# Block 2's output product by token block, with residual, norm and transposes beside it, and the first MLP product begun with the first token half

## What is computed

```
    h = rms_norm(x, norm_mix[l])
    x = x + hybrid_mixer(h, ...)          # ends with: return y @ w_out
    h = rms_norm(x, norm_mlp[l])
    x = x + jnp.square(jax.nn.relu(h @ w_up[l])) @ w_down[l]
    return rms_norm(x, norm_final)
```

## Time and profile before

| | us |
|---|---|
| median of 3 runs | 3333.64 (3332.24 to 3339.71) |
| the profiled execution | 3333.65 |
| its span in the trace | 3331.8 |
| PE busy | 3049.6 (92%) |
| DVE busy | 1804.0 (54%) |
| ACT busy | 1091.8 (33%) |
| POOL busy | 956.8 (29%) |

### The profile page before, as it was taken

How to read it: one execution, slowest core, us unless ns; L and a number is a source line. 1 busy time by engine, 2 the same in 40 slices (tenths; PEclk the granted TensorE clock), 3 DMA queues, 4 the chain that set the end, 5 groups by cost and what they waited for, 6 DMA issues and landing times.

```text
span 3331.8 us, 49239 instructions
## 1 busy us (share of the span) xinstructions
PE 3049.6 (92%) x20177; PEld 1927.5 (58%) x20394; DVE 1804.0 (54%) x2991; ACT 1091.8 (33%) x1912; POOL 956.8 (29%) x958
## 2 busy tenths in 40 slices
PE   7989988998779969997999999999998899999997
PEld 7449773885439646873555655654656644444443
DVE  2584892666489973767365265365353333333334
ACT  2352651664356634654122122222221310000001
POOL 2301383002203571012423322323222233333330
PEclk9997999999899989998999999999898899999998
DMA  7313231002102321003101111111102111111101
GB/s 241 126 57 118 77 137 54 30 11 102 67 13 77 115 89 49 14 28 128 51 26 38 51 38 39 38 39 51 39 13 102 39 51 51 51 51 51 51 26 57
DMA packets 49168, 207.19 MB, mean 62 GB/s; under 512 B 4488, under 2 KB 9776, under 8 KB 32304
## 3 DMA queue, kind: packets, MB, share of 16 engines
q1 hardware_dynamic: 42288, 195.63, 16.5%
q10 hardware_dynamic: 6656, 8.39, 0.8%
HBM read 187.22 MB, written 16.79 MB: 61 GB/s over the span
## 4 chain that ended last, share of the span: by engine, by line
PE 75%; DVE 15%; issue 4%; ACT 3%; DMA 1%; POOL 1%; DVEq 0%; SPq 0%; ACTq 0%; POOLq 0%
PE big L270 17%; PE big L271 17%; PE big L269 17%; PE banks L269 4%; PE banks L270 4%; PE banks L271 4%; PE banks L994 3%; DVE arena L1614 2%; PE banks L861 1%; DVE arena L1835 1%; PE big L548 1%; PE banks L548 1%; DVE arena L2004 1%; DVE arena L1817 1%; DVE arena L1949 1%
## 5 line engine op out<-in xcount | busy, mean ns | idle before, releaser
L511 POOL CAST w_hi<-stage 128x512 bf16<-128x512 f32 x432 | 284.7, 702 | 1880.5 <-PE big L271 1142.6
L518 POOL TENSOR_TENSOR w_lo<-stage,w_hi 128x512 bf16<-128x512 f32 x520 | 676.4, 1333 | 396.9 <-ACT w_hi L1129 396.2
L270 PE MATMUL big<-ht_lo,w_hi 128*128 128x512 bf16 x1381 | 526.6, 381 | 21.1 <-DVE ht_lo L1515 18.7
L271 PE MATMUL big<-ht_hi,w_lo 128*128 128x512 bf16 x1380 | 525.8, 381 | 1.4
L269 PE MATMUL big<-ht_hi,w_hi 128*128 128x512 bf16 x1359 | 517.7, 381 | 1.5
L269 PE MATMUL big<-w_hi,ht_hi 128*128 128x256 bf16 (+1 forms) x1274 | 383.8, 301 | 22.5 <-POOL w_lo L518 9.6
L271 PE MATMUL big<-w_hi,ht_lo 128*128 128x256 bf16 (+1 forms) x1276 | 384.2, 301 | 0.5 <-issue 0.2
L270 PE MATMUL big<-w_lo,ht_hi 128*128 128x256 bf16 (+1 forms) x1274 | 383.7, 301 | 0.6 <-issue 0.4
L269 PEld LDWEIGHTS big<-ht_hi,w_hi 128*128 128x128 bf16 x1408 | 140.1, 100 | 180.3 <-DVE ht_lo L1515 19.1
L271 PEld LDWEIGHTS big<-ht_hi,w_lo 128*128 128x128 bf16 x1408 | 138.4, 98 | 168.3 <-issue 3.8
L270 PEld LDWEIGHTS big<-ht_lo,w_hi 128*128 128x128 bf16 x1408 | 138.4, 98 | 162.1 <-issue 6.0
(11 more groups left out here) (319 smaller groups left out, 6095.8 us busy)
## 6 DMA issues: line engine op xcount, KB each, us to landing
stage<-in_w SPq DMA_DIRECT2D x130, 1024.0 KB, 4.8
arena<-in_w_ada SPq DMA_DIRECT2D x48, 512.0 KB, 4.2
arena<-in_x SPq DMA_DIRECT2D x16, 512.0 KB, 7.0
xs<-arena SPq DMA_DIRECT2D x16, 512.0 KB, 2.6
arena<-xs SPq DMA_DIRECT2D x16, 512.0 KB, 7.9
gt<-arena ACTq DMA_DIRECT2D x16, 256.0 KB, 2.5
arena<-gt ACTq DMA_DIRECT2D x16, 256.0 KB, 2.6
out_x<-arena SPq DMA_DIRECT2D x8, 512.0 KB, 2.6
```

What stands on the lines that cost most here:

```text
L270: pe.matmul(out, ah, bl, start=False, stop=False)
L271: return pe.matmul(out, al, bh, start=False, stop=stop)
L511: pool.tensor_copy(w_hi[:, n % RING, c0:c1], stage[:, n % RAW_RING, c0:c1]).then_inc(s_w_hi_split, mark(s_w_hi_split, n, q))
L518: ins = pool.tensor_tensor(w_lo[:, n % RING, c0:c1], stage[:, n % RAW_RING, c0:c1], w_hi[:, n % RING, c0:c1], ALU.subtract)
```

## The change

The output product goes by token block. Chunks o0 to o3 now hold a quarter of `w_out` each as 512 rows x 512 columns (in place of 1024 x 256), so that a token block's PSUM tile holds its whole row of 1024 outputs and takes 48 matmuls of 512 columns. Token blocks 0 and 1 are done first together: for both, the six k that belong to b = 0 to 2 come before the wait for the last tile of `Y2`, the two k of b = 3 behind it. Blocks 2 to 7 follow one by one. DVE adds a block's row, then normalises the block before it, into a new place (`X_TOK3`, since `Y2` is still read).

The first token half is turned in the middle of block 6, the second in the middle of up0, which is done in four parts (column tile 0 and 1 of the first token half, then of the second). The transposes go to the `c2` banks. The passes behind them are new and fewer: ACT scales from PSUM straight to `ht_hi`, DVE makes `ht_lo` from PSUM, gain and `ht_hi` in one instruction. On both engines the first half's passes stand ahead of block 5's step. SP's reload of x moves from behind o2's load to behind up1's. up0's tiles are in pool `big`; up1 starts pool `mlp` at its first tile.

```
-                if n == CHUNK_AT[(2, "o2")]:
+                if n == CHUNK_AT[(2, "up1")]:
 
                     sp.wait_ge(s_hgrn_dve, when(s_hgrn_dve, "y2_f", 3, 1))
...
@@
+            def turn_x(l, half, kps):
+
+                if kps[0] == 0:
+                    for j in range(4):
+                        pe.wait_ge(s_xn, when(s_xn, l, half * 4 + j))
+                for kp in kps:
+                    g = take(pe, "c2", "hx", l, half, kp)
+                    for kk in range(2):
+                        for j in range(4):
+                            k = 2 * kp + kk
+                            ins = pe.transpose(g[:, kk * 512 + j * P:kk * 512 + (j + 1) * P],
+                                               x_tok(l)[:, half * 4 + j, k * P:(k + 1) * P], ident)
+                    ins.then_inc(s_gemm, mark(s_gemm, "hx", l, half, kp))
+
+            def first_gemm(l, name, keys):
...
+                part(0, 0)
+                turn_x(l, 1, (0, 1))
+                part(1, 0)
+                turn_x(l, 1, (2, 3))
+                part(0, 1)
+                part(1, 1)
+                chunk_used(l if l < LAYERS else 2, name, s_gemm)
+
+            def out_tokens(l, names, yT, first_two, ready):
...
+                def part(t, g, p, c, ks=range(4)):
+                    w = chunk(l, names[p][c], 4)
+                    for k in ks:
+                        ins = mm3(pe, g[:, c * 512:(c + 1) * 512], [x[:, 4 * p + k, t * P:(t + 1) * P] for x in yT],
+                                  [x[:, k, :] for x in w], p == 0 and k == 0, p == 1 and k == 3)
+                    return ins
+
+                first = [take(pe, "big", "y", l, t) for t in range(2)]
+                first_two(part, first)
+                for t in range(2, NT):
+                    ready(t)
+                    g = take(pe, "big", "y", l, t)
+                    for q, (p, c) in enumerate(((0, 0), (0, 1), (1, 0), (1, 1))):
+                        if t == 6 and q < 3:
+                            turn_x(nl, 0, ((0, 1), (2,), (3,))[q])
+                        ins = part(t, g, p, c)
+                        if t == NT - 1 and q < 3:
+                            ins.then_inc(s_gemm, mark(s_gemm, "y_part", l, p, c))
+                            chunk_used(l, names[p][c], s_gemm)
+                    ins.then_inc(s_gemm, mark(s_gemm, "y", l, t))
+                chunk_used(l, names[1][1], s_gemm)
@@
-            pe.wait_ge(s_hgrn_dve, when(s_hgrn_dve, "y2_lo", 3, 1))
-            out_proj(2, Y2)
-            transpose_x(3)
-            pe.wait_ge(s_ht_lo, when(s_ht_lo, "all", 3))
-            for c, j in MLP:
+
+            def first_two(part, g):
+                pe.wait_ge(s_hgrn_dve, when(s_hgrn_dve, "y2_lo", 2, 1))
+                for p, ks in ((0, range(4)), (1, range(2))):
+                    for c in range(2):
+                        pe.wait_ge(s_w_split, when(s_w_split, CHUNK_AT[(2, f"o{2 * p + c}")]))
+                        for t in range(2):
+                            part(t, g[t], p, c, ks)
+                pe.wait_ge(s_hgrn_dve, when(s_hgrn_dve, "y2_lo", 3, 1))
+                for t in range(2):
+                    for c in range(2):
+                        ins = part(t, g[t], 1, c, range(2, 4))
+                    ins.then_inc(s_gemm, mark(s_gemm, "y", 2, t))
+
+            out_tokens(2, (("o0", "o1"), ("o2", "o3")), Y2, first_two, lambda t: None)
+            first_gemm(3, "up0", [("up", 0, 0), ("up", 0, 1)])
+            for c, j in MLP[1:]:
@@
+                    if l >= LAYERS:
+                        for kk in (k - 1, k):
+                            act.activation(ht_hi[:, kk, half * 512:(half + 1) * 512], g[:, kk % 2 * 512:kk % 2 * 512 + 512], ACT.Identity,
+                                           scale=GSL[l][:, 8 + kk:9 + kk], bias=GSL[l][:, kk:kk + 1]).then_inc(s_ht_hi, mark(s_ht_hi, l, half, kk))
+                        continue
@@
             for i in range(NT):
+                if i == 5:
+                    ht_half(3, 0)
                 act.wait_ge(s_x_y, when(s_x_y, "x", i))
...
@@
+                        for k in (2 * kp, 2 * kp + 1):
+                            dve.wait_ge(s_ht_hi, when(s_ht_hi, l, half, k))
+                            dve.scalar_tensor_tensor(ht_lo[:, k, half * 512:(half + 1) * 512], g[:, k % 2 * 512:k % 2 * 512 + 512], GSL[l][:, 8 + k:9 + k],
+                                                     ht_hi[:, k, half * 512:(half + 1) * 512], ALU.mult, ALU.subtract).then_inc(s_ht_lo, mark(s_ht_lo, l, half, k))
@@
             for i in range(NT):
-                dve.wait_ge(s_gemm, when(s_gemm, "y", 2, 3, 3))
-                normalise(3, i, XR[:, i, :])
-            ht_part(3)
+                if i == 5:
+                    ht_half(3, 0)
+                dve.wait_ge(s_gemm, when(s_gemm, "y", 2, i))
+                dve.wait_ge(s_x_in[i], when(s_x_in[i], 2, i))
+                dve.tensor_tensor(XR[:, i, :], XR[:, i, :], tile("big", "y", 2, i)[:, :], ALU.add).then_inc(s_x_y, mark(s_x_y, "x", i))
+                freed(s_x_y, "y", 2, i)
+                if i:
+                    normalise(3, i - 1, XR[:, i - 1, :])
+            normalise(3, NT - 1, XR[:, NT - 1, :])
+            ht_half(3, 1)
```

More of the change, by code:

```diff
@@ L333, in build, with x_tok @@
         HF += [RBC[:, 0:512], RBC[:, 512:1024]]
+        X_TOK3 = fl(16384, 8192).rearrange("p (t d) -> p t d", t=NT)
+        def x_tok(l):
+            return X_TOK3 if l == 3 else X_TOK
         HFW = fl(at - 256 - 1024, 1024)
@@ new lines, in first_gemm, with part @@
+            def first_gemm(l, name, keys):
+                pe.wait_ge(s_w_split, when(s_w_split, CHUNK_AT[(l if l < LAYERS else 2, name)]))
+                w = chunk(l if l < LAYERS else 2, name, KT)
+                g = [take(pe, "big", *key) for key in keys]
+                def part(ct, half):
+                    for k in range(KT):
+                        if ct == 0:
+                            pe.wait_ge(s_ht_lo, when(s_ht_lo, l, half, k))
+                        ins = mm3(pe, g[ct][:, half * 512:(half + 1) * 512], [x[:, k, ct * P:(ct + 1) * P] for x in w],
+                                  [x[:, k, half * 512:(half + 1) * 512] for x in hT], k == 0, k == KT - 1)
+                    if half:
+                        ins.then_inc(s_gemm, mark(s_gemm, *keys[ct]))
+                part(0, 0)
[5 more added lines that the diff above has]
+                chunk_used(l if l < LAYERS else 2, name, s_gemm)
@@ new lines, in out_tokens @@
+            def out_tokens(l, names, yT, first_two, ready):
+                nl = l + 1
+                def part(t, g, p, c, ks=range(4)):
[18 more added lines that the diff above has]
+                chunk_used(l, names[1][1], s_gemm)
@@ L1435, in _ @@
                             act.wait_ge(s_rs_lo, when(s_rs_lo, j - 1, n))
-                        evac(RT[n], ACT.Relu, "up", j, n, pool="mlp")
+                        evac(RT[n], ACT.Relu, "up", j, n, pool="mlp" if j else "big")
                         if j >= 2:
```

78 lines of the change are left out of this document (48 added, 30 removed).

## The result

The changed kernel takes 3299.97 us, median of 4 runs (3297.0 to 3302.55), beside 3336.68 us (3332.24 to 3339.76) for the kernel before on the same chip: ratio 0.9891, with a 95% interval of 0.9873 to 0.9908. In a second comparison it took 3299.47 us against 3338.03 (0.9886, 0.9871 to 0.9900). The forecast was 3295.6 in a range of 3290 to 3305. The profiled execution took 3301.58 us, its span is 3299.8.

The account below looks back on a forecast made before the run. PE bounds the kernel, busy 3049.6 of 3331.8 us. Savings of 14.6 us (product with its turn) and 23.4 (norm, turns, up0) make 38.0: span 3293.8, plus 1.85 for the execution, 3295.6 us; range 3290 to 3305, own range 3291 to 3300.

Parts of the forecast that it names:

- Part 1: While PE waits for Y2's last tile, 72 output-product matmuls (15.5 us) run, ending 0.6 us before it arrives.
- the rival by the shared port pair: In the DVE chain before Y2's last tile, one POOL subtraction could hold it up once, giving 3297.2 us.
- The term for the clock: After each of PE's two sparse stretches, the slow start costs about 2 us; both go, already in the sum.
- Part 2: After Y2's last tile arrives, the remaining 312 product matmuls take 67.3 us, with no wait for x.
- Part 3: First half's 32 transposes inside block 6 take 4.2 us without waiting; block 5's add has 1.7 us cover.
- Part 4: up0 with the second half's 32 transposes ends at 2628.3; up1 begins at 2629.7 after a 1.4 us wait.
- A: The passes behind the transposes don't fit under the product; up to 13 us come back, 3300 to 3309; chance 0.13.
- B: The 72 matmuls wait for Y2's last tile after all; 15.5 us return, 3311; chance 0.04.
- C: x or up0 arrives late, 1 to 6 us in all, 3297 to 3301; chance 0.08 for more than 3 us.
- D: Granted clock gives way in the 680 us of MLP; 5.6% at 0.50 eats the 38 us, 10% makes 3364; chance 0.02.

Follow-up runs that it names:

- second profile: The changed kernel as it is, profiled once more: 675.54 us from the last gate's eviction to a late weight split; 3299.47 us median in that comparison.
- the idle matmuls: The kernel before with 72 unread matmuls ahead of the wait for Y2's last tile: 710.12 us from last gate's eviction to a late weight split, 2.88 less.
- the kernel with the undone fill: The changed kernel with the wait for Y2's last tile ahead of the 72 matmuls: 693.74 us from last gate's eviction to a late weight split, 18.20 more.
- the last one: The changed kernel without its two buffer waits, given 140 idle matmuls in the mixer: 3276.92 us against 3296.64 without them, ratio 0.9818 to the kernel before.

## Why the prediction came out right, point by point

**Time from the gate.** The forecast's steps, counted from 2514.19, beside those of after, counted from 2519.42:

| step | forecast | after |
|---|---|---|
| first product matmul | 1.6 | 1.5 |
| o3 split | 6.8 | 6.8 |
| first matmul behind the last tile | 17.7 | 17.7 (second profile) |
| product's last matmul done, with the first turn | 89.2 | 88.7 |
| up0 starts | 89.2 | 90.2 |
| up1 starts (before: 153.4) | 115.5 | 115.8 |

So the saving up to up1 is 37.6 us against 38.0 forecast, and 0.2 us more is lost in the 560 us behind it. PE being the bound to the end, every microsecond was kept, as said.

**Part 1** held to a few tenths. PE had 0.5 us to spare ahead of the last tile (forecast 0.6), and POOL beside DVE's reciprocal cost that nothing. The timeline of DVE in after, to be read beside the earlier trace rows:

```profile
2523.06 6.55 DVE L2124 RECIPROCAL arena<-arena 128x1024 f32<-128x1024 f32 x1 [9.19 <-ACT arena L1467]
...
2535.84 1.23 DVE L2137 TENSOR_TENSOR arena<-arena 128x1024 bf16<-128x1024 f32 x1 [1.12 <-ACT arena L1507]
```

POOL's subtraction ran from 2521.70 to 2526.19, three microseconds of it beside the reciprocal, which took 6.55 us, as ever. POOL was done before the two-input steps began at 2529.65. So the rival by the shared port pair, which the Trainium skill ("SBUF — State Buffer", "SBUF: two separate sides") describes, had no place to act here. A slower norm beside POOL came further on, harmlessly: the norms of blocks 6 and 7 took 1.64 and 1.45 us beside POOL's subtraction, where the others took 0.75. The row of block 6 stands below, with one of the others.

```profile
2564.56 0.75 DVE L1581 TENSOR_SCALAR arena<-arena,small 128x1024 f32<-128x1024 f32 x1
...
2609.42 5.40 POOL L522 TENSOR_TENSOR w_lo<-stage,w_hi 128x512 bf16<-128x512 f32 x4
2609.50 1.64 DVE L1581 TENSOR_SCALAR arena<-arena,small 128x1024 f32<-128x1024 f32 x1
```

The term for the clock was right: about 2 us for each slow start, where the kernel before lost 2.1 us behind the first hole, by the idle matmuls, and 1.8 us in up0 (22.52 us for 96 matmuls that take 20.7 at full clock). How long the lower level lasts differs: it cost 2.5 us in the kernel with the undone fill. The term entered the sum only as a reason, not as a number: the sum subtracts the whole old stretch from the new one.

**Part 2** held. x landed 3.3, 7.7 and 9.0 us (least, median, most) behind its issue and no matmul waited for it; the adds start 10.36 us apart.

**Part 3** had the right structure, with one number too large. A group of sixteen transposes takes 1.75 us and one of eight 0.87 at full clock with matmuls around, 0.109 us each; I took 1.05 for eight, a row measured between waits, whose length has an end of the last instruction in it. 64 transposes are 7.0 us, not 8.4. The tight place, block 5's add behind the passes of the first half, came out at 1.6 us of cover (forecast 1.7):

```profile
2593.44 1.42 DVE L1591 SCALAR_TENSOR_TENSOR ht_lo<-banks,small,ht_hi 128x512 bf16<-128x512 f32 x2 [2.04 <-ACT ht_hi L1110]
2594.78 1.21 DVE L2144 TENSOR_TENSOR arena<-arena,big 128x1024 f32<-128x1024 f32 x1
```

The add ends at 2595.99, and PE starts on the tile at 2597.61.

**Part 4** has a step that failed, hidden in the total. For up0's start I checked only its weights: "Chunk up0 takes o0's slot". These were in time, at 2607.24 against 2607.91. What I missed is that `first_gemm` takes both `big` tiles ahead of its first matmul, and that one of them is block 7's, whose add begins only when the product ends. That wait is 1.51 us. The order of the instructions would have shown the buffer, had I read it there as I did at up1. The wait at up1 was forecast at 1.4 us and is 1.2. The missed 1.5 us and the transposes' 1.4 us cancel, so the total is closer than its terms.

**Rivals.** A (passes not under the product) didn't come: they cost nothing in after, and 6.65 us when their cover is taken away, half of the 13 that I had as its upper end. B would have been 18.2 us by the experiment, not 15.5. C's late arrivals didn't occur. D, the clock giving way in the longer unbroken run, neither: 1.00 over 624 us.

**The total.** 3299.97 us is 4.4 us above the forecast. From the gate to the end the change gives 37.2 us in place of 38.0, which is 0.8 of them. The rest lies ahead of the gate, where the profiled execution of before, from which I forecast, came 5.2 us earlier than that of after with the same code. In the two comparisons the single runs of the kernel before lie between 3331.30 and 3339.89 us. That my own range of 3291 to 3300 held the median, by 0.03 us, is luck; I had not looked at how far executions differ.

## What to carry to other kernels

When PE has to wait for the last part of an operand, give it first the matmuls that need only the parts already there. It needs accumulation tiles that stay open and weights that are split early, so look at every queue that feeds them: here one DMA's place on SP was worth 25 of 37 us. At each start of a product ask both questions, when its weights are there and who still holds its tiles; I asked only one. Measure a late change from an instruction that both kernels share just ahead of it, when the part before scatters: that told 3 us where medians of four runs could not. The same care is due where the change is early: an experiment's one profile can be 8 us ahead by chance before its edit begins, as in the last one.

## What the runs showed of the hardware

Identical code ahead of the gate ran at granted clocks from 0.67 to 0.92 in the same stretch of 44 us, where PE does small fp32 matmuls between waits of up to 1.9 us. 140 idle matmuls of 512 columns in those waits held it at 1.00 and took 3296.64 us down to 3276.92, 0.6% for a few instructions, in a kernel that had 92% PE busy and looked full. The profiles show 14.5 us of that in the mixer; the spread between executions stayed. The Trainium skill ("TensorE: Matmul & The Clock Gate", "HAM oscillation — how this bites in real kernels") describes such going back and forth between the levels for products that wait for DMA; here it is the same with waits for DVE, by the rows above. Behind the idle hole the fall cost 2.1 us in one pair of kernels and 2.5 us in another, by two experiments that priced it in opposite directions. And transposes of fp32 follow the clock as matmuls do: sixteen took 1.75 us among matmuls at 1.00, and 3.65 at 0.50.
